# Hybrid decoder layer: the normalised rows of x reach the projection from a turned copy, and 1 / rms as a row through DRAM

## The reference

```python
h = rmsnorm(x, ln_gain)          # x * rsqrt(mean(x*x) + EPS) * gain, per position
z = h @ w_in                     # 1024 x 4608: q, k, v, gate A, recurrent input, recurrent gate
y_attn = rmsnorm(swa_sink_attention(rope(q), rope(k), v) * silu(g_attn))   # window 128, 4 kv x 4 q heads
y_lru  = rmsnorm(rg_lru(causal_conv4(x_lru)) * silu(g_lru))
x = x + concat([y_attn, y_lru]) @ w_out
out = rmsnorm(x, final_gain)
```

## Time and profile before

| | |
|---|---|
| median of 3 runs | 1377.39 us (1375.57 to 1378.08) |
| profiled execution, its own time | 1375.05 us |
| its span, first to last instruction | 1373.4 us |
| granted TensorE clock, mean | 0.997 |
| busy: PE, DVE, ACT, POOL | 98%, 71%, 62%, 16% |
| DMA, mean over the span | 177 GB/s |

### The profile page before, as it was taken

The page is one execution under the profiler, slowest core; times in us unless marked ns, Lnnn a source line. Parts: engine busy times, 40 slices in busy tenths (PEclk is TensorE's granted clock), DMA queues, the critical chain, the costliest instruction groups (busy, mean ns, idle before and its releaser), DMA issues.

```text
span 1373.4 us, 22283 instructions
## 1 busy us (share of the span) xinstructions
PE 1352.7 (98%) x6756; PEld 1107.8 (81%) x6756; DVE 969.1 (71%) x1668; ACT 845.5 (62%) x1729; POOL 217.6 (16%) x247
## 2 busy tenths in 40 slices
PE   8999999999999999999999999999989999999998
PEld 7787878788888888888888888888867888888886
DVE  5898989868686877868787767878686544434442
ACT  7878797967777685867777585766764221222120
POOL 2021212122130312113031212213020000000000
PEclk9999999999999999999999999999999999999999
DMA  9766868654544555454555655354535423223220
GB/s 343 248 233 231 281 214 293 230 188 173 183 175 180 202 185 197 161 187 172 185 186 184 227 201 208 145 197 167 190 114 194 138 86 97 98 85 121 62 92 31
DMA packets 98289, 243.22 MB, mean 177 GB/s; under 512 B 8112, under 2 KB 43056, under 8 KB 98224
## 3 DMA queue, kind: packets, MB, share of 16 engines
q1 hardware_dynamic: 91200, 217.79, 46.3%
q0 software_dynamic: 7024, 24.65, 4.5%
HBM read 179.49 MB, written 62.91 MB: 176 GB/s over the span
## 4 chain that ended last, share of the span: by engine, by line
PE 79%; DVE 2%; DMA 1%; ACT 1%; issue 1%; DVEq 0%; POOL 0%; ACTq 0%; POOLq 0%
PE ring L1544 45%; PE acc_b L223 12%; PE ring L223 11%; PE ps_tv L1607 3%; PE ps_s L1583 2%; PE ps_tv L1594 2%; PE ring L1621 1%; PE ps_tv L1583 1%; PE ring L1631 1%; DMA y_scratch<-ya 1%; DMA w_raw<-w_out_d 0%; PE ring L1556 0%; PE acc_b L1994 0%; DVE cu L1340 0%; DVE wo_rest L169 0%
## 5 line engine op out<-in xcount | busy, mean ns | idle before, releaser
L1544 PE MATMUL ring<-split,w_hi 128*128 128x512 f32 x2288 | 716.9, 394 | 1.3 <-DVE w_lo L1079 0.7
L1544 PEld LDWEIGHTS ring<-split,w_hi 128*128 128x128 f32 x2288 | 421.3, 188 | 97.1 <-issue 6.7
L1544 PE MATMUL ring<-split,w_lo 128*128 128x512 f32 x1144 | 446.4, 390 | 0.0
L1544 PEld LDWEIGHTS ring<-split,w_lo 128*128 128x128 f32 x1144 | 214.7, 188 | 45.9
L663 POOL TENSOR_SCALAR_AFFINE_SELECT p_hi_c<-p_hi 128x512 fp32r<-128x512 f32 x64 | 41.9, 654 | 521.1 <-ACT p_hi L891 520.8
L883 ACT ACTIVATE p_sb<-s_sb,smax 128x129 f32<-128x129 f32 x256 | 99.6, 392 | 0.6
L1836 ACT ACTIVATE w_hi<-res 128x1024 fp32r<-128x1024 f32 x15 | 15.9, 1060 | 132.3 <-DVE res L1909 132.3
L223 PE MATMUL acc_b<-wo_rest,y_own 128*128 128x512 f32 x384 | 91.3, 394 | 5.0 <-DVE rms L1894 4.6
L1340 DVE SCALAR_TENSOR_TENSOR cu<-xl,prm,cu 128x512 f32<-128x512 f32 x96 | 72.1, 751 | 29.2 <-ACT cu L910 24.2
L223 PE MATMUL ring<-split,y_own 128*128 128x512 f32 x384 | 91.5, 392 | 0.0
L223 PEld LDWEIGHTS acc_b<-wo_rest,y_own 128*128 128x128 f32 x384 | 72.6, 190 | 20.9 <-DVE rms L1894 4.7
(11 more groups left out here) (249 smaller groups left out, 2418.9 us busy)
## 6 DMA issues: line engine op xcount, KB each, us to landing
w_hi<-w_split_scratch SPq DMA_DIRECT2D x108, 512.0 KB, 3.2
w_lo<-w_split_scratch SPq DMA_DIRECT2D x108, 512.0 KB, 4.3
w_raw<-w_tiles_d SPq DMA_DIRECT2D x36, 512.0 KB, 4.6
w_split_scratch<-w_hi SPq DMA_DIRECT2D x36, 512.0 KB, 5.1
w_split_scratch<-w_lo SPq DMA_DIRECT2D x36, 512.0 KB, 5.9
y_scratch<-hs POOLq DMA_DIRECT2D x32, 256.0 KB, 6.2
y_scratch<-ya POOLq DMA_DIRECT2D x16, 512.0 KB, 6.1
rows<-y_scratch SPq DMA_DIRECT2D x8, 1024.0 KB, 7.8
```

The lines of the kernel that those rows point to most:

```text
L1544: last = mm(bank(r), w[:, i % WSLOTS, k, :], h[:, par, k, :], start=(k == 0 and j == 0), stop=(k == KC - 1 and j == 2))
```

## The change

The host passes a second input `x_turned`: x in blocks of 128 positions, each with columns as rows (partition p holds x[t, c*128+p] at [c, t]). SP loads it to `xt`, where the gain row stood, in addition to `xb`. 1 / rms is one value per position, so for `xt` it must vary along the free axis: after `invert_x`, SP stores the 128 values of `xs[:, 3]` to a DRAM row and reads that row back into every partition (`rs_row`). `norm_x` is now eight 128x128 instructions xt * gain (a value per partition) * rs_row, and `high_x` and `low_x` read `xt` from SBUF. PE's `turn_x` and the two ring places are gone; the bank of every other ring place, and the place in front of it, are the same as before. `load_x` now waits for `low_x` in place of `turn_x`, and the wait of PE ahead of KVG asks for `h_low`.

```diff
+BANK = [0, 1, 2, 3, 0, 1, 2, 3, 0, 3, 0, 1, 2, 3]
+IN_FRONT = [max(s for s in range(r - NR, r) if BANK[s % NR] == BANK[r]) for r in range(NR)]
...
-            sp.dma_start(gain_row, ln_gain.broadcast_to([P, D])).then_inc(gain_in, 16)
...
             def load_x(g, q):
 
                 sp.dma_start(xb, x[0, bass.ds((g + (q + 1) * KV) * P, P), :]).then_inc(*x_in.one())
+                sp.dma_start(xt, x_turned[bass.ds(g + (q + 1) * KV, 1), :, :, :].rearrange("o p k t -> p (o k) t")
+                             ).then_inc(*x_in.one())
...
                 load(GL1)
+                if q < NQUART - 1:
+
+                    sp.wait_ge(*x_rs.at(n, 1))
+                    sp.wait_ge(*x_norm.at(n, 0))
+                    sp.dma_start(rs_dram.rearrange("o p -> p o"), xs[:, 3:4]).then_inc(*rs_kept.one())
+                    sp.wait_ge(*rs_kept.at(n, 1))
+                    sp.dma_start(rs_row[:, :], rs_dram.broadcast_to([P, P])).then_inc(*rs_in.one())
...
                 if x_follows(q, nxt_par != par):
-                    sp.wait_ge(*ring_ready.at(n, R_XT1 + 1))
+                    sp.wait_ge(*h_low.at(n, 2))
                     load_x(following, q + (nxt_par != par))
...
-            def high_x(dst, col, half, ps, ready, done):
-                act.wait_ge(*ready)
+            def high_x(n, dst, col, half):
+                part = slice(half * 4, half * 4 + 4)
+                act.wait_ge(*x_norm.at(n, 1))
                 act.sem_inc(settled, 1)
+                nc.scalar.activation(dst[:, part, bass.ds(col, P)], xt[:, part, :], ACT.Copy).then_inc(*h_high.one())
...
+            def invert_x(n):
+                dve.wait_ge(*x_root.at(n, 0))
+                dve.wait_ge(*rs_kept.at(n, 0))
+                nc.vector.reciprocal(xs[:, 3:4], xs[:, 2:3]).then_inc(*x_rs.one())
+
             def norm_x(n):
-                dve.wait_ge(*x_root.at(n, 0))
-                nc.vector.reciprocal(xs[:, 3:4], xs[:, 2:3]).then_inc(*x_rs.one())
-                dve.wait_ge(*x_rs.at(n, 1))
-                stt(out=xb, in0=xb, scalar=xs[:, 3:4], in1=gain_row, op0=ALU.mult,
-                    op1=ALU.mult).then_inc(*x_norm.one())
...
+                dve.wait_ge(*x_in.at(n, 0))
+                dve.wait_ge(*rs_in.at(n, 1))
+                for c in range(KC):
+                    last = stt(out=xt[:, c, :], in0=xt[:, c, :], scalar=prm[:, C_GAIN, c:c + 1], in1=rs_row[:, :],
+                               op0=ALU.mult, op1=ALU.mult)
+                last.then_inc(*x_norm.one())
...
+            def low_x(n, dst, hi, col, half):
+                dve.wait_ge(*h_high.at(n, half + 1))
+                part = slice(half * 4, half * 4 + 4)
+                at = (slice(None), part, bass.ds(col, P))
+                nc.vector.tensor_tensor(dst[at], xt[:, part, :], f(hi[at]), ALU.subtract).then_inc(*h_low.one())
...
                 conv(0)
+                if q < NQUART - 1:
+                    invert_x(n)
                 low_gates()
...
-                def turn_x():
-                    pe.wait_ge(*x_norm.at(n, 1))
-                    for half in range(2):
-                        pe.wait_ge(*bank_free(n, R_XT0 + half))
-                        for k in range(4):
-                            c = half * 4 + k
-                            last = nc.tensor.transpose(bank(R_XT0 + half)[:, k * P:(k + 1) * P],
-                                                       xb[:, c * P:(c + 1) * P], ident[:, :])
-                        last.then_inc(*ring_ready.one())
...
                 turn_p(0)
-                if q < NQUART - 1:
-                    turn_x()
                 score(3)
...
                 if nxt_par != par:
-                    pe.wait_ge(*ring_dve.at(n, FREED_BY_DVE.index(R_XT1) + 1))
+                    pe.wait_ge(*h_low.at(n, 2))
```

More of the change, by code:

```diff
@@ L391, in phase_a @@
         ring_dve = signal("ring_dve", len(FREED_BY_DVE))
-        x_in = signal("x_in", 1, 16, ahead=1)
+        x_in = signal("x_in", 2, 16, ahead=2)
+        rs_kept = signal("rs_kept", 1, 16)
+        rs_in = signal("rs_in", 1, 16)
         x_sq = signal("x_sq", 1, ahead=1)
@@ L473, in bank_free @@
         def bank_free(n, r):
-            before = (r - RING) % NR
-            late = 0 if r >= RING else 1
+            before = IN_FRONT[r] % NR
+            late = 0 if IN_FRONT[r] >= 0 else 1
             if before in FREED_BY_ACT:
@@ L1006, in body @@
                     for half in range(2):
-                        high_x(h_hi[:, 1 - par], g * P, half, bank(R_XT0 + half),
-                               ring_ready.at(n, R_XT0 + half + 1), h_high.one())
+                        high_x(n, h_hi[:, 1 - par], g * P, half)
                 elif g > 1:
@@ L1352, in silu_l @@
                               op0=ALU.add, op1=ALU.mult)
-                    if u and q == NQUART - 1:
-                        ins.then_inc(*ring_dve.three())
-                    else:
-                        ins.then_inc(*ring_dve.one())
+                    ins.then_inc(*ring_dve.one())
                 def one_less(u):
@@ L1430, in body @@
                     for half in range(2):
-                        low_x(h_lo[:, 1 - par], h_hi[:, 1 - par], g * P, half, bank(R_XT0 + half),
-                              h_high.at(n, half + 1), ring_dve.one())
+                        low_x(n, h_lo[:, 1 - par], h_hi[:, 1 - par], g * P, half)
                 elif g > 1:
@@ L1545, in project @@
                                   start=(k == 0 and j == 0), stop=(k == KC - 1 and j == 2))
-                if turned:
-                    last.then_inc(*ring_ready.one())
-                else:
-                    last.then_inc(*ring_ready.three())
+                last.then_inc(*ring_ready.one())
             def turn_v(n):
@@ L1646, in body @@
                 turn_p(0)
-                if q < NQUART - 1:
-                    turn_x()
                 score(3)
-                project(n, GL1, par, split, q < NQUART - 1)
+                project(n, GL1, par, split)
                 weigh_v(0)
@@ L2102, in laid_out @@
             gates[:, half, :, :, (j + half) % 2, :] = blocks[:, :, half].transpose(0, 2, 1, 3)
-    return {"channel_params": np.stack([by_unit(v) for v in rows], axis=1),
+    x_turned = np.asarray(inputs["x"])[0].reshape(NTOK, P, KC, P).transpose(0, 3, 2, 1)
+    return {"x_turned": x_turned, "channel_params": np.stack([by_unit(v) for v in rows], axis=1),
             "out_gains": np.concatenate([by_unit(inputs["attn_out_gain"]), by_unit(inputs["lru_out_gain"])], axis=1),
```

47 lines of the change are left out of this document (18 added, 29 removed).

## The result

The changed kernel takes 1435.13 us (median of 4 runs, 1431.85 to 1436.55), the kernel before beside it 1377.3: a ratio of 1.0417 (1.0405 to 1.043), 4.2% slower. The prediction was 1371.0 us, 0.5% faster. The profiled execution took 1434.7 us, its span 1433.1 us, its mean granted clock 0.977.

What follows compares the result with a forecast made beforehand. PE was taken to set the pace except in quarter 0, where an ACT-DVE loop does. Gains of 5.2 + 1.2 + 0 = 6.4 us off 1375.05 gave 1368.7, plus 2.3 for the median 1371.0 us; range 1366 to 1377.

Steps and rivals of the forecast that it cites:

- The row through DRAM: Quarters 1 and 2: store issued at 364.6, row there at 371.4, DVE coming at 371.05; hidden.
- the reserve of 1.2 us: Quarters 1 and 2: DVE 0.9 us late at norm_x against an allowed 2.1, so hidden by 1.2 us.
- The rival "slower": Nine bodies: row late by the whole queue, landing at 376.0, DVE 5.4 us late; about 1401 us, chance 0.10.
- The allowance: Behind norm_x: DVE may be 2.1 us late at silu_a(0), ahead of GL1, before PE feels it.
- the falsifier: Wrong if DVE waits over 1.6 us for rs_row, PE waits for silu_a(0) before GL1, or quarter 0's period moves.
- high_x and low_x "within 0.05 us each": On DVE: the same 128x512 copies with SBUF as source, durations within 0.05 us, before work that isn't waited for.
- the three waits ahead of KVG: Last bodies of the quarters (3, 7, 11): new PE waits for low_x, 0.3 to 0.7 us each.
- The turns: Eight transposes, 0.87 us of PE a body: 5.2 us from six middle bodies, 1.2 from last ones, 0 from bodies 0-2.
- norm_x: On DVE: eight instructions for one, less the reciprocal, -0.15 to +0.9 us, taken as +0.5 and covered.
- Quarter 0: Bodies 0 to 2: an ACT, DVE, ACT loop without PE, its period staying 64.2 us; no gain.
- The keeps: Quarter 0: last keep lands about 148 instead of 144, ACT 1.2 us late against 1.35 idle; no cost.
- The chances: Faster 0.76, within 0.2% 0.13, slower 0.11; forecast 0.60, rivals 0.09, 0.13, 0.10 and 0.08.

Runs made afterwards that it cites:

- e3: Changed kernel with 1 / rms made at the body's start and, in quarters 1 and 2, SP's store and broadcast ahead of load(GA0): 1429.12 us, ratio 1.0389.
- e8: Kernel before plus the DRAM detour alone, with a store of 512-byte pieces in quarter 1 and a read of 128 different rows in quarter 2: 1383.18 us.
- e9: Kernel before plus the detour alone; quarter 1 broadcasts another, long finished row, quarter 2 stores the row as one 512-byte piece: 1391.09 us.
- e4: Changed kernel without the detour: PE makes the row by a matmul against ident, ACT copies it, reciprocal at the body's start: 1380.84 us, ratio 1.0032.
- e6: e4 with low_x moved behind top(3), and in a quarter's last body ahead of lru_scan(0): 1371.25 us, ratio 0.9964.
- e7: Kernel before with two of the eight transposes per body, low_x still from PSUM: 1371.58 us, ratio 0.9966.
- e10: e6 with norm_x as one 128x1024 instruction, one chunk's gain standing for all: 1373.04 us, ratio 0.9971.
- e1: Changed kernel without the store, the broadcast and their waits, rs_row filled with ones: 1379.35 us, ratio 1.0022.
- e2: Changed kernel with store, wait and broadcast on POOL at the start of its body, in all three quarters: 1418.24 us, ratio 1.0314.
- e5: Kernel before, turns kept, plus only the detour and the reciprocal behind conv(0), norm_x waiting for the unused row: 1429.74 us, ratio 1.039.

## Why the prediction was wrong, by its steps

- **The row through DRAM** is the step that failed, and by nearly all of the loss. It had the store land at 368.3 to 369.8, 3.7 to 5.2 us after its issue, "another 1.5 us" over the weights'. It takes 8.5 us (median), whatever stands ahead of it (e3) and because of its 4-byte pieces (e8, e9). The broadcast had 2.0 to 4.0 and takes 5.3, because it reads what those pieces wrote. 3.3 to 4.8 us from the one and 1.3 to 3.3 from the other are more than the reserve of 1.2 us. No row of the trace had a store in small pieces; the 1.5 us on top were drawn from rows of 512 KB, and the 2.0 for the broadcast from one of 256 KB, as if fewer bytes landed sooner, while loads of 8 and 36 KB in the same view had taken 4.4 and 6.3.
- **The rival "slower"** had the mechanism, with a chance of 0.10 and 1401 us: a store 3 us over the weights, DVE 5.4 late, 3.3 beyond its allowance. DVE was 7.3 + 0.7 = 8.0 late, and PE waited 5.1 on average in eight bodies, not nine.
- **The allowance** named silu_a(0), ahead of GL1, as the tightest, and the falsifier asked for a wait there. PE waits at turn_p(0), for softmax_b(0), which was named as queued but not priced. With a delay of 8 us the first consumer in order decides, not the one with the smallest reserve. The reserve of softmax_b(0) was 2.9 us, and 8.0 - 2.9 is the wait of 5.1 (DVE's and PE's timelines before; the first ends at 375.38):

```profile
374.69 0.69 DVE L1301 TENSOR_TENSOR p_sb<-p_sb,sden 128x512 f32<-128x512 f32 x1
378.25 0.60 PE L1594 MATMUL ps_tv<-ident,p_sb 128*128 128x128 f32 x4
```

- **The clock** stood in no term. Behind each wait of 5 us PE loses 1.9 to 2.6 us more, 18.5 in all, nearly half of what the waits themselves cost (40.9). A rival with a wait of PE has to carry it.
- **high_x and low_x "within 0.05 us each"** is the second failed step, for low_x: 1.28 us became 2.4 to 2.8, next to POOL's multiplication. It looked at the instruction alone and not at what runs beside it. This, its consequences and the place of low_x are 9.6 us (e4 to e6) and cancel the gain. With the earlier low_x the three waits ahead of KVG, forecast at 0.3 to 0.7 us each, are gone; with the slow one they are up to 1.5.
- **The turns** were right: 0.87 us a body on PE (e7: 60.7 us of a forecast 60.7 for six of eight). That they gain nothing in bodies 0 to 2 fits: e7 is 5.4 us faster, where 7.5 were forecast if they counted there, too.
- **norm_x** was taken at +0.5 (the reciprocal taken off) and is 2.19 - 1.28 - 0.15, about +0.7, inside its bounds and hidden (e10).
- **Quarter 0** was to keep 64.2 us. In e1 its bodies 1 and 2 take 67.1 and 65.8. Part is low_x, part a stretch of low clock in body 1 (windows of the changed kernel, the body and the stretch):

```profile
89.25:156.40 67.15, 63.95 (x312) 50.53 (x312) 60.81 (x105) 52.95 (x108) 13.07 (x13) 0.97 0.68 242
118.00:122.00 4.00, 4.00 (x11) 3.13 (x12) 3.77 (x6) 3.77 (x7) 0.00 (x0) 0.57 0.54 47
```

It stands behind PE's wait for silu_l(0) of that body, which had no such stretch in the profile of before, and GA0 takes 7.2 us there in e1 in place of 5.65. The keeps do land later, as said: ACT waits for them up to 4.1 us, not the 1.2 of the forecast, but DVE has no gap by it. How much each has in the 4.4 us of the two bodies wasn't separated; e6 has them at 65.6 and 66.8. But not all of it is the change's: e7, which has low_x from PSUM and one copy of x, has the same stretch of low clock at 118.7, and its bodies 1 and 2 take 66.0 and 64.6, 2.2 us more than in the profile of the kernel before. That profile was a quick one: the median of that kernel's runs is 2.3 us above it.
- **The chances** by outcome (0.76, 0.13, 0.11) and by rival (0.60 + 0.09 + 0.08 = 0.77, 0.13, 0.10) differ by 0.01.

With a row that costs next to nothing and low_x away from POOL, the total comes out at what was forecast, 1371.25 us, by way of two more edits that the change didn't have, and partly by luck. In the profiles of e6 and of the kernel before, quarters 1 and 2 give 5.3 us where the forecast had 6.2 for them (PE now makes the row, 0.27 us a body, and the bodies at their end no longer wait for low_x). Quarter 3 gives 0.3 us a body (60.44 against 60.7), which no term had and no run explains. Quarter 0 is 3.8 us longer than in the profile of before, but it is 4.2 longer in e7, too, so this is not shown to be the change.

## What to carry to other kernels

Price a DMA by the size of its pieces, and not only by its bytes: one value per partition written to DRAM was the slowest transfer of this kernel, and a small matmul against the identity turned it into a row without leaving the core. When an operand moves from PSUM to SBUF, look at which engine works on SBUF beside that instruction, and move one of the two. When a wait of PE is priced, add what the clock takes after it.

## What the runs showed of the hardware

- 128 pieces of 4 bytes to DRAM, all into the same 512 bytes: 8.5 us (7.1 to 9.7; after), 8.5 with the queue of weights empty (e3), 7.7 from POOL (e2). 128 pieces of 512 bytes: 3.9 (e8). One piece of 512: 3.3 (e9).
- A broadcast of a row just written in 4-byte pieces: 5.3 us (3.6 to 6.1; after); of the same row just written in one piece: 2.8 (e9).
- A DVE subtraction of 128x512 with both inputs in SBUF beside a POOL multiplication of the same shape: 0.68 us becomes up to 1.82, and POOL's 1.30 becomes 1.78 (before, after, e1).
- At PE waits of 4.8 to 5.6 us the granted clock fell 1.2 to 2.7 us before the wait's end and stayed at its lower level for 6.8 us, in eight bodies of eight (after); PE lost 1.9 to 2.6 us behind the wait. In e5 waits of 3.7 to 4.5 us had the same 6.8 us, but three others (2.1, 4.5 and 4.8) only 3.4, which began up to 1.0 us behind the wait's end; in e8 four waits of 1.2 to 2.0 us had no such stretch.
- A matmul with a single column broadcast as its weights and the identity as the moving operand gives that column as a row in all partitions, in 0.27 us for each of its two records (e4).
